# PEER layers: gathers of four picks for 32 tokens each, weighed with 128x32 tiles in four column groups

## What is computed

```
q = (h @ w_q)                          # 8 heads, two halves of 128 each
s1, s2 = q_half . sub_keys             # 128 scores a half; the best 16 of each
best 16 of the 16 x 16 sums a head     # expert = 128 * i + j
gate = softmax(best 16)                # for each head
y = sum over heads, picks: gate * gelu(h . u[expert]) * v[expert]
x = x + g * y
```

## Time and profile before

| | us |
|---|---|
| median of 3 runs | 2351.16 (2350.08 to 2351.41) |
| profiled execution: span from its first to its last instruction | 2348.5 |
| what lies around the span, taken as median less span | 2.7 |
| busy PE / DVE / ACT / GpSimd in the span | 1898.6 / 1336.1 / 327.4 / 558.9 |
| moved by the DMA engines | 894.78 MB, of which 536.90 MB by the gathers |
| first PEER layer, first gather issued to last weighing | 856 to 1519 |
| second PEER layer | 1673 to 2340 |

### The profile page before, as it was taken

One profiled execution on the slowest core, in us unless ns is written; L12 is line 12 of the kernel. 1 busy time (PEld: TensorE's weight loads), 2 busy tenths in 40 slices (PEclk: granted clock), 3 DMA queues, 4 the chain that ended last, 5 costly groups with the idle time before them and its releaser, 6 DMA issues. The chain is left out here.

```text
span 2348.5 us, 24798 instructions
## 1 busy us (share of the span) xinstructions
PE 1898.6 (81%) x9231; PEld 1016.4 (43%) x9231; DVE 1336.1 (57%) x3275; ACT 327.4 (14%) x822; POOL 558.9 (24%) x568
## 2 busy tenths in 40 slices
PE   6998766666679799998877777799999988777776
PEld 4665433333367464444323232285655443222322
DVE  3533000000065558767877886656677678778866
ACT  1052000000021430010000000113310100000001
POOL 1000000000000114434434344200134344344332
PEclk9999888888889899999999999999999999999999
DMA  9987999999997459999999999896599999999997
GB/s 384 412 259 308 430 428 428 430 429 428 425 332 308 176 227 398 421 421 421 417 421 417 413 416 422 347 362 249 210 417 421 421 421 414 421 414 420 409 421 323
DMA packets 147192, 894.78 MB, mean 381 GB/s; under 512 B 18461, under 2 KB 30589, under 8 KB 63869
## 3 DMA queue, kind: packets, MB, share of 16 engines
q0 software_dynamic: 73728, 536.90, 55.3%
q1 hardware_dynamic: 73340, 356.25, 38.2%
HBM read 889.68 MB, written 3.42 MB: 380 GB/s over the span
## 5 line engine op out<-in xcount | busy, mean ns | idle before, releaser
L2000 PE MATMUL psum<-sb_area 128*128 128x512 f32 x2048 | 980.1, 616 | 236.9 <-DVE sb_area L2755 232.6
L2781 DVE CUSTOM_DVE_ANT_0 sb_area<-sb_area 128x1024 f32<-128x1024 f32 x512 | 626.0, 1223 | 279.3 <-DMA sb_area<-in_peer_uv,sb_peer_e 276.6
L815 POOL DMA_INDIRECT sb_area<-in_peer_uv,sb_peer_e x512 | 541.1, 1057 | 1006.7 <-PE psum L2000 733.1
L2000 PEld LDWEIGHTS psum<-sb_area 128*128 128x128 f32 x2048 | 375.6, 194 | 721.1 <-DVE sb_area L2755 372.4
L1650 PE MATMUL psum<-sb_area 128*32 128x256 f32 x2048 | 172.1, 510 | 130.4 <-DMA sb_area<-in_moe_w_gu 128.4
L2283 DVE COPY sb_area<-psum 128x128 f32<-128x128 f32 x32 | 9.3, 292 | 391.4 <-PE psum L1662 391.4
L1233 ACT ACTIVATE sb_small<-sb_small 128x2 f32<-128x2 f32 x258 | 52.5, 204 | 1143.6 <-DVE sb_small L2781 1143.6
L2755 DVE SCALAR_TENSOR_TENSOR sb_area<-sb_ident,sb_small,sb_area 128x128 f32<-128x128 f32 x512 | 156.4, 346 | 50.6 <-ACT sb_small L1233 45.9
L1650 PEld LDWEIGHTS psum<-sb_area 128*32 128x32 f32 x2048 | 82.7, 145 | 219.5 <-DMA sb_area<-in_moe_w_gu 142.3
L1350 PE MATMUL psum<-sb_area 128*128 128x256 f32 x784 | 174.4, 384 | 3.2 <-DVE sb_area L2117 3.2
L795 POOL TENSOR_SCALAR_AFFINE_SELECT sb_area<-sb_area 128x256 f32<-128x256 f32 x1 | 0.4, 409 | 726.7 <-DVE sb_area L2587 726.7
(11 more groups left out here) (375 smaller groups left out, 1374.1 us busy)
## 6 DMA issues: line engine op xcount, KB each, us to landing
sb_area<-in_moe_w_gu SPq DMA_DIRECT2D x30, 4096.0 KB, 33.4
sb_area<-in_ada_w SPq DMA_DIRECT2D x72, 1024.0 KB, 12.8
sb_area<-in_moe_w_dn SPq DMA_DIRECT2D x32, 2048.0 KB, 24.1
sb_area<-in_peer_w_q SPq DMA_DIRECT2D x8, 2048.0 KB, 7.9
sb_area<-in_sb_w_in SPq DMA_DIRECT2D x6, 2048.0 KB, 21.2
sb_area<-in_odd_w_in SPq DMA_DIRECT2D x6, 2048.0 KB, 11.0
sb_area<-in_even_w_in SPq DMA_DIRECT2D x5, 2048.0 KB, 13.9
sb_area<-in_moe_w_gu SPq DMA_DIRECT2D x4, 2048.0 KB, 21.3
```

The source lines that it names most:

```text
L815: pool.indirect_dma_start(uv_rows[s], None, rows, bass.IndirectOffsetOnAxis(ap=peer_e[:, m:m + 1], axis=0)).then_inc(named(f"uv_loaded{s}" ...
L2000: last = pe.matmul(ps[:, 4 + 2 * t + half, :], diag[:, s, :], uv_rows[s][:, D + half * HALF:D + (half + 1) * HALF], start=(k == 0), stop=( ...
L2781: dve.tensor_tensor_reduce(uv_rows[s][:, 0:D], uv_rows[s][:, 0:D], h_tok[:, m // P, :], 1.0, 0.0, ALU.mult, ALU.add, dots[:, m % BODY:m % ...
```

## The change

A gather still brings 128 rows of 8 KB, but of four picks for 32 tokens each: partition block p (32 partitions) of step m holds pick (4 * (m // 4) + p) of the 32 tokens of block m % 4. The picks and gates of a unit are moved between partition blocks to fit this (`move_picks`, `move_gates`: 16 small copies each on ACT; for unit 0 the picks by DVE and ACT, 8 copies each and head). The diagonal tile becomes 128x32: one matmul sums four picks of 32 tokens into the 32 PSUM partitions of block m % 4, and four successive steps use the four column groups of the array. The dot needs h repeated: for each token block a tile whose four partition blocks hold the same 32 rows (`turn_rep`, 32 matmuls each, four for each token tile, and `copy_rep`, 128x1024). BATCH is 4, and the last four picks go singly. Of the second token tile, the repeated rows take the place of the queries, so all searches have to be over by then: they start at picks 8, 28, 42, 56, 70, 84 and 98, two steps to a pick. ACT does `exp_gates` and `move_picks` ahead of the gelu of the batch that holds pick start + 7, `move_gates` ahead of that of start + 10. The products of PE stand four to a pick in picks 8 to 45, where they stood one or two to a pick in picks 2 to 101 (`project_step`, of 256 columns) and before. Constants of earlier stages share memory with a tile of repeated rows. Cut to its core:

```diff
+BLOCK = 32
+BLOCKS = P // BLOCK
 BODY = 32
-BATCH = 2
+BATCH = 4
 UNIT = 32
 UNITS = T // UNIT
-SEARCH_AT = 8
-EXP_AT = 26
-PROJECT_AT = {2: 2, 3: 36}
-SECOND_AT_PICK = BATCH
+SEARCH_START = {1: 8, 2: 28, 3: 42, 4: 56, 5: 70, 6: 84, 7: 98}
+SEARCH_PACE = 2
+PICKED_AFTER = 7
+GATED_AFTER = 10
+STEPS = 4
+SECOND_AT_PICK = 2
 FIRST_AT_PICK = 8
-QUICK_AT = 20
+FIRST_TAKE_AT = 16
 LOW_ROWS_AT = 5
-TAKE_AT = {2: 36, 3: 68}
-KEYS_AT = {2: 37, 3: 69}
-COPY_AT = {2: 40, 3: 72}
-LATE_AT = 70
-ROW_AT = 112
-ROW_TAKE_AT = 116
+PROJECT_AT = {2: 16, 3: 26}
+LATE_AT = 38
+KEYS_AT = {25: (2, 0), 37: (3, 0), 46: (0, 1), 50: (1, 1), 54: (2, 1), 58: (3, 1)}
+TAKE_AT = {2: 24, 3: 36}
+LATE_TAKE_AT = 48
+COPY_AT = {28: (2, 0), 40: (3, 0), 48: (0, 1), 52: (1, 1), 56: (2, 1), 60: (3, 1)}
+TOKENS_AT = [62, 66, 70, 74]
+TOKENS_OUT_AT = [64, 68, 72, 76]
+ROW_AT = 80
+ROW_TAKE_AT = 84
 OPEN_AT = 240
...
-        diag = view(K + 2048, RING, P)
-        gate = view(K + 3072, NT * PEER_HEADS, PEER_K)
+        gate = view(K + 2304, NT * PEER_HEADS, PEER_K)
+        gate_q = view(K + 3584, T)
...
-        key_score = view(K + 5744, NT * HP, NKEYS)
+        key_score = view(K + 5744, HP, NKEYS)
+        h_rep = [[view(at, D) for at in (2048, K + 7792, K + 8816)] + [early], [view(16384 + D * b, D) for b in range(BLOCKS)]]
...
                     if m % UNIT == 0 or m == PEER_K:
                         pool.wait_ge(named("experts_made"), experts_at(L, m))
+                        if m < UNIT:
+                            pool.wait_ge(named("picks_found"), picks_at(L, 0) + 2 * (m // PEER_K) + 1)
...
+                def copy_rep(t, b):
+
+                    act.wait_ge(named("ht_psum"), 4 + NT * BLOCKS * L + BLOCKS * t + b + 1)
+                    bank = 4 if t == 0 else 2 * (b % 2)
+                    act.activation(h_rep[t][b][:, :], ps[:, bank:bank + 2, :].rearrange("p b n -> p (b n)"), ACT.Copy
+                                   ).then_inc(named("h_tok_ready"), 1)
+
+                def move_picks(u, first_head, count, first_block):
+
+                    first = u * GK + first_head * PEER_K
+                    nk = count * PEER_K
+                    act.wait_ge(named("picks_found"), picks_at(L, u) + (0 if count == GH else 2 * first_head))
+                    for b in range(first_block, BLOCKS):
+                        for p in range(BLOCKS):
+                            last = act.activation(peer_e[BLOCK * p:BLOCK * (p + 1), first + b:first + nk:BLOCKS],
+                                                  pick_e[BLOCK * b:BLOCK * (b + 1), first + p:first + nk:BLOCKS], ACT.Copy)
+                    last.then_inc(named("experts_made"), 1)
+
+                def move_gates(u):
+
+                    act.wait_ge(named("gate_parts"), 2 * (UNITS * L + u) + 2)
+                    flat = gate.rearrange("p h k -> p (h k)")
+                    for b in range(BLOCKS):
+                        for p in range(BLOCKS):
+                            last = act.activation(gate_q[BLOCK * p:BLOCK * (p + 1), u * GK + b:(u + 1) * GK:BLOCKS],
+                                                  flat[BLOCK * b:BLOCK * (b + 1), u * GK + p:(u + 1) * GK:BLOCKS], ACT.Copy)
+                    last.then_inc(named("gates_out"), 1)
...
                 copy_keys(0, (0,))
+                move_picks(0, 0, 1, 2)
                 if split:
-                    copy_tok(0)
-                    copy_tok(1)
+                    copy_rep(0, 0)
+                    copy_rep(0, 1)
                     square_part(stage, 1, 0)
+                    move_picks(0, 1, 1, 2)
                     exp_gates(0)
                     act.activation(warm[:, :], ones[:, 0:1], ACT.Sqrt)
                     square_part(stage, 1, 1).then_inc(ssq_done, 1)
                     act.wait_ge(var_done, x_updates(stage) + 1)
                     act.activation(std[:, 1:2], var[:, 1:2], ACT.Sqrt).then_inc(std_done, 1)
                     act.activation(warm[:, :], ones[:, 0:1], ACT.Gelu_apprx_tanh)
+                    move_gates(0)
+                    copy_rep(0, 2)
+                    copy_rep(0, 3)
...
                 else:
                     norm_second(stage)
-                    copy_tok(0)
-                    copy_tok(1)
+                    copy_rep(0, 0)
+                    move_picks(0, 1, 1, 2)
                     exp_gates(0)
                     act.activation(warm[:, :], ones[:, 0:1], ACT.Gelu_apprx_tanh)
+                    copy_rep(0, 1)
+                    move_gates(0)
+                    copy_rep(0, 2)
+                    copy_rep(0, 3)
                     act.wait_ge(proj_done, groups_here[0][0] + 1)
                     take_tile(0, 1, range(4), proj_out)
...
-                    u, at = b * BATCH // UNIT + 1, b * BATCH % UNIT
-                    if u < UNITS and at == EXP_AT:
-                        exp_gates(u)
+                    for u, start in SEARCH_START.items():
+                        if (start + PICKED_AFTER) // BATCH == b:
+                            exp_gates(u)
+                            move_picks(u, 0, GH, 0)
+                        if (start + GATED_AFTER) // BATCH == b:
+                            move_gates(u)
                     if b * BATCH < LAST:
                         gelus(b * BATCH, BATCH)
...
+                def turn_rep(t, b):
+
+                    bank = 4 if t == 0 else 2 * (b % 2)
+                    if t == 0 and b:
+                        pe.wait_ge(named("h_tok_ready"), 4 + NT * BLOCKS * L + b)
+                    if t and b >= 2:
+                        pe.wait_ge(named("h_tok_ready"), 4 + NT * BLOCKS * L + BLOCKS + b - 1)
+                    tokens = slice(t * P + BLOCK * b, t * P + BLOCK * (b + 1))
+                    for k in range(KC):
+                        for p in range(BLOCKS):
+                            last = pe.matmul(ps[BLOCK * p:BLOCK * (p + 1), bank + k // 4, k % 4 * P:(k % 4 + 1) * P],
+                                             hT[:, k, tokens], ident[:, :], start=True, stop=True, skip_group_check=True)
                     last.then_inc(named("ht_psum"), 1)
...
+                    turn_rep(0, 0)
                     key_scores(0, 0, range(2, GQ))
+                    turn_rep(0, 1)
                     out_products(*last_out, 1, range(KC)).then_inc(proj_done, 1)
                     pe.wait_ge(w_loaded[second % 3], w_turns(second))
-                    for f in range(4):
-                        last = tile_products(1, 0, f, range(KC))
-                    last.then_inc(named("head_projected"), 1)
+                    tile_products(1, 0, 0, range(KC))
+                    tile_products(1, 0, 1, range(KC))
+                    turn_rep(0, 2)
+                    tile_products(1, 0, 2, range(KC))
+                    tile_products(1, 0, 3, range(KC)).then_inc(named("head_projected"), 1)
+                    turn_rep(0, 3)
...
+                    turn_rep(0, 0)
                     pe.wait_ge(hT_low, rows + 2)
                     pe.wait_ge(hT_high, rows + 2)
-                    for f in range(4):
-                        last = tile_products(0, 1, f, range(KC))
-                    last.then_inc(proj_done, 1)
-                    tile_products(1, 0, 2, range(KC // 2))
-                    key_scores(0, 1)
-                    tile_products(1, 0, 2, range(KC // 2, KC))
+                    tile_products(0, 1, 0, range(KC))
+                    tile_products(0, 1, 1, range(KC))
+                    turn_rep(0, 1)
+                    tile_products(0, 1, 2, range(KC))
+                    turn_rep(0, 2)
+                    tile_products(0, 1, 3, range(KC)).then_inc(proj_done, 1)
+                    turn_rep(0, 3)
...
+                def weigh(first, count):
+
+                    pe.wait_ge(named("diag_made"), batches_at(L, first + count - 1))
+                    for m in range(first, first + count):
+                        pe.wait_ge(named(f"uv_loaded{m % RING}"), 16 * ((L * T + m) // RING + 1))
                     for half in range(2):
-                        last = pe.matmul(ps[:, 4 + 2 * t + half, :], diag[:, s, :], uv_rows[s][:, D + half * HALF:D + (half + 1) * HALF],
-                                         start=(k == 0), stop=(k == P - 1), skip_group_check=True)
-                        if m == T - 1 and half == 0:
-                            last.then_inc(named("y_low_done"), 1)
-                    last.then_inc(named("v_used"), 1)
+                        for m in range(first, first + count):
+                            s, t, b = m % RING, m // P, m % BLOCKS
+                            last = pe.matmul(ps[BLOCK * b:BLOCK * (b + 1), 4 + 2 * t + half, :], diag[:, s, :],
+                                             uv_rows[s][:, D + half * HALF:D + (half + 1) * HALF],
+                                             start=(m % P < BLOCKS), stop=(m % P >= P - BLOCKS), skip_group_check=True)
+                            if m == T - 1 and half == 0:
```

(51 more changed lines are left out.)

159 lines of the change are left out of this document (63 added, 96 removed).

## The result

| | kernel before | kernel after |
|---|---|---|
| median of 4 runs | 2351.11 us | 2544.88 us (2536.68 to 2546.34) |
| ratio, 95% interval | | 1.0823 [1.0806, 1.0841] |
| profiled execution, its span | 2350.08 us, 2348.5 | 2536.68 us, 2534.9 |

The forecast was 2456 in a range from 2370 to 2515. The sign was right and the size was not: 194 us against 105.

A forecast was written before the change was run, and what follows sets the result against it. DMA gathers bound the kernel, so only pauses of the DMA engines cost time: 2348.5 + 84 for searches + 21 for starts = 2453.5 us span, 2456 with 2.7 around it; range 2370 to 2515.

The forecast's parts named there:

- Outside the searches ... Nothing is lost or gained there: Picks without search steps: a batch's slots refill before the ring runs dry, 1.4 to 3.1 us over; no time lost.
- the chain's terms: Last landing of a batch to new data: 0.36 + 1.5 + 0.5 + 1.7 + 2.7 = 6.8 us, against 9.9 of transfers.
- PE to the first free slot: Within a batch of four picks: first slot free after somewhat over half of PE's 2.8 us, 1.7 us.
- PE's part: Products of four picks on narrow tiles: 2.8 us, by a ratio of 2.6 from the experts' tiles; doubled at half clock.
- The searches: Two steps a pick: DVE burst 4.3, ACT stall 3.5, gates 0.5, less 2.3 hidden: 6.0 a unit, 84 us both layers.
- ACT's copies: The 16 small copies each for picks and gates: 0.11 us apart, 1.7 us for 16 (ends 1.4 and 3.7).
- The starts: Start of each layer, repeats of h and copies delay the first free slots: 9 us first layer, 12 us second.
- Hidden: Rival: bursts and starts cost under 5 us in all; 2351 us; chance 0.07.
- faster: Rival: earlier free slots close dips in the DMA rate, 0.8% of 1270 us gained; 2341 us; chance 0.07.
- mild: Rival: the searches' lag is half, since the ring holds more than counted; 14 x 1.5 + 10, 2382 us; chance 0.08.
- The column groups don't work side by side: Rival: with 512 columns, PE takes 4.6 us a batch more and repeats 8.9 us; 2523 us; chance 0.08.
- What the prediction said would blame PE: Sign against the forecast: DMA holes spread evenly over all 256 picks, not one to a search early in each layer.

The follow-up runs named there:

- experiment 7: Kernel after with PE's products of a batch pick by pick, not half by half over the four picks: 2544.44 us, 1.0829.
- experiment 4: Kernel after with 12 of the 16 ACT copies of a unit's gates left out, most weights then wrong: 2545.87 us, 1.0833.
- experiment 8: Kernel after with ACT's exponential of the gates and copies of the picks one pick later: 2520.92 us, 1.0737.
- experiment 5: Kernel after with batches of two and searches at one step a pick: 2377.24 us, 1.0117.
- experiment 10: Kernel before, batches of two, with each search at two steps a pick and the exponential at 16: 2358.83 us, 1.0053.
- experiment 1: Kernel after with batches of two instead of four: 2452.02 us, 1.0438.

## Why the prediction was right in sign and too small

**The bound.** Right. The gathers bound both kernels, and the time is what the DMA engines lose by running dry.

**The step that failed: "Outside the searches ... Nothing is lost or gained there", with 1.4 to 3.1 us of slack in the ring.** Batches of four cost 93 us by the medians and 83 in the profiled executions (186.7 less 103.4), of which 25.1 and 22.8 come after pick 112 and 18.5 and 19.4 among the searches. The forecast, which puts this term at nothing, is 2456, and the kernel with batches of two took 2452. That they are 4 us apart is partly luck: that kernel lost 65 us among the searches where 84 was forecast and 43 in the starts where 21 was (part of the first search runs there), and won 5 back behind pick 112. Of the chain's terms, in the batch shown above:

- dot to diagonals: 1405.87 to 1407.38, 1.51 us (1.50 forecast), right.
- four diagonals: 0.79 to PE's start, not 0.5.
- PE to the first free slot: 3.89, not 1.7. Two errors in one. The clock fell, as the prediction had considered and then halved by taking the middle. And "somewhat over half" was wrong: groups side by side end together, so no slot is free before nearly all of the work is done (experiment 7 shows it in both orders).
- issue to landing and landing to dot: forecast 5.5 and 0.36, from the earlier trace rows. The landing records put it otherwise: there the last is at 889.79, 5.9 after the issue and 0.02 ahead of the dot. In the batch shown the last is at 1420.53, 8.5 after the issue at 1412.06, and again 0.03 ahead of the dot. The 0.36 that the prediction put between landing and dot is in neither. The first issue takes 1.70 instead of 0.94, and the new transfers begin while some DMA engines still work on old ones. Landing is when the slowest engine is done; the first is done 1.8 us earlier (1404.04 against 1405.85), and the GB/s row falls with it. I had counted the ring's content from the landing, as if all engines ended with it.

Sum: 0.02 + 1.51 + 0.79 + 3.89 + 8.47 = 14.7 us from the last landing of one batch to the first of the batch that takes the slots freed, where five landings at 2.48 allow 12.4. The 2.3 us too many are the 0.9 and 1.4 that the two steps between batches show. The prediction's own terms gave 9.6. This batch is dearer than most: it loses 0.9 us, and the 25.1 us in 36 batches are 0.7 each.

**PE's part.** Forecast 2.8 us for four picks from a ratio of 2.6. Measured 1.92 at a clock of 0.92 and 3.64 on the slow one. The eight wide instructions of the earlier trace rows take 3.70 for two picks, 0.46 each; a wave of four narrow ones takes 1.92 / 4 = 0.48. So on the fast clock the groups give nearly four times, and my ratio from the experts' tiles was the wrong row to take. By the Trainium skill, "TensorEngine Tiling (Array Packing)", section "Theoretical Speedup", up to four times is the promise; by it, as an estimate, the batch would take 1.9 us. On the fast clock the trace agrees. The gain in PE's time is real, 980 to 451 us of `weigh`, and worth nothing, since PE was not the bound.

**The searches.** Forecast 84 us; going from two steps to one gave back 75 by the medians with batches of two, and 64 with batches of four. About right in size. DVE was busy 71% there (213.51 of 300) and not near 90: the holes are its waits. The stall at the last pick of a batch was named and measured at 5.31 against 4.7. The burst of 5.8 us alone costs the old kernel 0.8 a unit. That points to the sum of burst and stall, as the prediction had added them, but no run parts it from searches that follow each other after 14 picks. The prediction's slack of 2.3 us was too small for batches of two and too large for batches of four. Two gathers fewer in flight are 5.0 us, about the difference between a ring that nearly hides a burst of 5.8 and one that loses in every batch. That reading is argued from the numbers: no run changed the number of slots.

**ACT's copies.** Dearer than forecast, 0.215 us against 0.11, and yet cheaper in effect: leaving out 12 of 16 of those of the gates gained nothing (experiment 4), those of the picks cost where they stand ahead of a gelu that DVE waits for (experiment 8).

**The starts.** Forecast 21 us, 24 left in the kernel of experiment 5 (11.5 and 12.4). The ninth gathers came 10.5 and 18 later against 9 and 16. Right to some 15%. A repeat took 3.50 and 1.95 us against 3.4.

**The rivals.** "Hidden", "faster" and "mild" are out. "The column groups don't work side by side" named 2523 with the wrong mechanism: they do, at four times. What the prediction said would blame PE, holes over all 256 picks, came in part: 390 GB/s behind the searches, beside 330 among them. It is PE's late release in large batches and not its busy time.

**A version for use.** None here beats the kernel before. With batches of two and one step a pick the change costs 1.2%, nearly all in the starts.

## What to carry to other kernels

In a ring that feeds a DMA-bound loop, count the slots that are in flight when a batch's slots come free, and the time from the last landing to the next landing; a batch of half the ring lost 93 and 122 us of 2350 here, though no compute engine was the bound. An engine made faster by packing can release its buffers later: with batches of two the first slot came 2.3 us after PE's start with full tiles (1441.48 to 1443.74 in the kernel before) and 3.9 with narrow ones (experiment 1), since packed pieces end together and the idle engine's clock falls. Work in a burst that hides by itself, as in experiment 10, need not hide beside a wait in a queue; that the two add up is argued here, not shown.

## What the runs showed that was not expected

- The column groups' order in the program made no difference: pick by pick or half by half, 16 narrow instructions took 3.66 and 3.64 us on the slow clock, and no slot came free earlier.
- Keeping PE busy with useless matmuls made the kernel faster by 28 us. The rows show a granted clock of 0.92 beside 0.57. The Trainium skill, "TensorE: Matmul & The Clock Gate", says in its part on the HAM clock gate that an idle PE drops to half the clock; the trace agrees, 3.64 against 1.92 us, a factor of 1.9.
- A gather issued into a ring that is nearly drained needed 8.1 and 8.5 us until its last landing (1401.14 to 1409.25, 1412.06 to 1420.53), against 5.9 at the start of the layer before, where nothing older was left in the queues.
- 32-partition copies of 8 columns on ACT start 0.22 us apart, though other small ACT instructions start 0.11 apart.
